# The first and last stages of a four-mixer block: input norm and final norm in the token layout, earlier parameter loads and scan operands

## The chip, the cores and the metric

One core of a Trainium2 chip. The metric is device microseconds of one execution; the kernel before takes 4182.87 us (median of 3 runs, 4181.97 to 4183.15). Everything is float32, and each matmul of that type appears in the trace as two records, a transposition as one.

## The reference

The input x has 1024 tokens of 1024 channels. The block is a long chain; only its two ends matter here:

```
h = rmsnorm(x, norm_g[0]);  proj = h @ s5_w_in;  branch, gate = split(proj)      # the head
y = s5_mixer(branch, A, log_dt, B, C, D)        # 64 groups, 64 complex states each, scan over time
x = x + ((gelu(y) * sigmoid(..)) * silu(gate)) @ s5_w_out
...                                             # gMLP, delta rule, attention, MLP, three more mixers
x = x + mixed @ w_out                           # last projection
out = rmsnorm(x, final_norm_w)                  # the tail
rmsnorm(x, g) = x * rsqrt(mean(x*x over the channels) + 1e-6) * g
```

## The kernel before

The residual lives in SBUF as `c.X`, [128 partitions, 8 blocks, 1024 tokens]: channels on the partitions. Inputs and outputs in memory have tokens in rows, so both ends are turned on TensorE. PSUM is two tensors of four banks: `products`, used as two groups of 128x1024 by turns (`start_group` waits until the group two before was read, `take_group` waits for the product, `taken` for its reading), and `others`. The engines run one written-out program each, phase after phase, with semaphores between them. SP issues the weight blocks (512 KB, eight places in a ring), ScalarE's queue the parameters and x, GpSimd's queue the scratch stores and loads and the output.

The head. ScalarE issues 13 small vector loads (L3909), then the eight tiles of x (L643), which one semaphore counts. TensorE (L654) waits for all of x and fills each product group with one block of 128 channels; ScalarE and VectorE copy the groups to `c.X` by turns (L661, L671), ScalarE squares each block (L453) and VectorE adds the squares up (L460). `rms_phase` multiplies the sum with a matrix of 1/1024 (`mean_of_total`, L489 and L493), takes Ln (L187) and Exp (L190) of 128x1024 elements and scales the eight blocks (L520). Before all that VectorE makes seven level masks (L3921 to L3928), three instructions each.

`s5_input_phase` multiplies eight blocks of the first half of `s5_w_in` (L161 in `product_ct`). TensorE first turns the state parameters' rows (L722, L723), which wait for a VectorE copy (L777) that stands behind the eight scalings. ScalarE evacuates a block (L753), GpSimd stores it to `branch_scratch` (L759). Meanwhile VectorE works out the discretised state parameters (L773 to L875) from B, C and the rest, which ScalarE's queue loads in this phase (L702 to L716).

`s5_scan_phase` has eight items. For item i VectorE makes operands (`s5_pq_done`), TensorE turns them (L985) and makes the masks' products (L997), ScalarE copies both (L1033, L1038), and TensorE needs the branch from scratch memory, in another layout, for L1006. Records of the gate's product (L962) are filled in between: one product, one product, then fourteen. GpSimd loads the branch (L926, eight DMAs per item), stores and loads the mask matrices (L940, L944). It starts on the loads of items 0 and 1 only after all eight blocks are stored, since an area of the work tensor is shared; ScalarE too waits for all eight stores before L1033.

The tail. The last projection's blocks are added to the residual (L1275), squared and summed as above; then `rms_phase` scales `c.X` in place, and `store_phase` turns it back (L3660, eight transpositions to a group), ScalarE and VectorE copy the groups by turns (L3665, L3670), and GpSimd issues the eight output tiles (L3676).

## Time and profile before

| | |
|---|---|
| median of 3 runs | 4182.87 us |
| profiled execution | 4190.77 us |
| its span, first to last instruction | 4189.0 us |
| mean granted TensorE clock | 0.97 |
| TensorE busy | 3933.0 us, 94% |
| VectorE, ScalarE, GpSimd busy | 1731.7, 895.1, 566.4 us |

A timeline row gives the start, the time from the first start to the last end of the merged instructions, the engine, the line, the operation with its tensors (output before input) and sizes, the count, and in brackets the idle time before it with what ended it. PE is TensorE's matmul, PEld its weight load, DVE VectorE, ACT ScalarE, POOL GpSimd; a q behind a name is the engine's DMA issuing. The granted clock is 1.00 at 2.4 GHz and 0.50 at 1.2 GHz.

### The profile page before, as it was taken

The page shows a single profiled execution, that of the slowest core. Times are in us where ns is not written, and L with a number is a line of the kernel's source. Part 1 is how long each engine was busy: PE and PEld are TensorE (multiplying, and loading weights), DVE is VectorE, ACT ScalarE, POOL GpSimd, SP SyncE. Part 2 cuts the span into 40 slices and gives each one's busy share as a digit, 9 for nine tenths or more (in the row PEclk, how much of TensorE's full clock was granted, in tenths as well). Part 3 has the DMA queues.
Part 4 walks back from the last instruction along what each step waited for, and adds up shares of the span by engine and source line. Part 5 has one row for each costly group of instructions (what it writes and reads, how often), then busy time and mean ns, then how long its engine had stood idle before and what let it go on. Part 6 is the DMA issues. An engine that isn't in the chain of part 4 may idle for free.

```text
span 4189.0 us, 32294 instructions
## 1 busy us (share of the span) xinstructions
PE 3933.0 (94%) x12935; PEld 1991.0 (48%) x12935; DVE 1731.7 (41%) x2512; ACT 895.1 (21%) x1033; POOL 566.4 (14%) x609
## 2 busy tenths in 40 slices
PE   5999999999899999977999999999899999899998
PEld 2455444544344776444444444444345554444553
DVE  5476433433333543144343332423445553424433
ACT  2111211111362222244130000000233430321122
POOL 0144110121000321022121221221000000000000
PEclk8998999999999999988999999999999999999998
DMA  3233111111011110200021111111101001003101
GB/s 111 79 69 84 48 40 51 40 50 41 15 35 41 26 41 16 71 21 21 10 67 44 40 50 41 40 49 42 31 26 31 26 10 46 13 13 98 31 13 43
DMA packets 291105, 174.50 MB, mean 42 GB/s; under 512 B 24095, under 2 KB 281998, under 8 KB 290702
## 3 DMA queue, kind: packets, MB, share of 16 engines
q1 hardware_dynamic: 253008, 126.47, 11.1%
q0 software_dynamic: 10000, 24.39, 2.2%
q10 hardware_dynamic: 27950, 21.58, 1.7%
q8 instruction: 104, 1.70, 0.2%
q14 instruction: 43, 0.35, 0.0%
HBM read 159.20 MB, written 13.21 MB: 41 GB/s over the span
## 4 chain that ended last, share of the span: by engine, by line
PE 54%; DVE 3%; ACT 2%; issue 1%; DMA 1%; POOL 0%; ACTq 0%; DVEq 0%
PE products L326 23%; PE products L2880 8%; PE products L161 7%; PE products L2893 3%; PE others L2959 2%; PE products L2081 1%; PE products L179 1%; PE products L534 1%; PE others L2275 1%; PE products L2244 1%; PE products L2090 1%; PE products L3408 1%; PE products L3407 1%; DMA work<-gates_scratch 1%; PE others L1492 1%
## 5 line engine op out<-in xcount | busy, mean ns | idle before, releaser
L2880 PE MATMUL products<-normed,weights 128*128 128x512 f32 (+2 forms) x704 | 318.5, 602 | 5.0 <-DVE normed L520 5.0
L161 PE MATMUL products<-normed,weights 128*128 128x512 f32 x704 | 312.5, 604 | 6.9 <-DVE s_small L3619 4.0
L326 PE MATMUL products<-gate,s_small 128*128 128x512 f32 x704 | 313.0, 592 | 0.0
L326 PE MATMUL products<-work,s_small 128*128 128x512 f32 x544 | 243.1, 593 | 0.3 <-DVE row L382 0.3
L344 POOL TENSOR_TENSOR s_small<-weights 128x512 f32<-128x512 f32 x60 | 79.5, 1325 | 1137.4 <-PE products L326 965.9
L326 PE MATMUL products<-normed,s_small 128*128 128x512 f32 x512 | 230.1, 592 | 2.3 <-DVE row L382 2.3
L356 ACT ACTIVATE s_small<-products 128x512 f32<-128x512 f32 x60 | 35.9, 599 | 861.1 <-PE products L326 861.1
L161 PEld LDWEIGHTS products<-normed,weights 128*128 128x128 f32 x704 | 135.0, 194 | 176.6 <-issue 165.3
L326 PEld LDWEIGHTS products<-gate,s_small 128*128 128x128 f32 x704 | 133.8, 190 | 168.4 <-issue 168.4
L326 PE MATMUL products<-normed,weights 128*128 128x512 f32 x448 | 203.7, 598 | 3.0 <-ACT normed L1023 3.0
L2880 PEld LDWEIGHTS products<-normed,weights 128*128 128x128 f32 (+2 forms) x704 | 125.4, 185 | 162.0 <-issue 160.3
L161 PE MATMUL products<-residual,weights 128*128 128x512 f32 x416 | 181.2, 593 | 0.9 <-ACT work L1593 0.9
L3676 POOL DMA_DIRECT2D out_dram<-work x8 | 4.3, 542 | 1210.0 <-ACT work L3665 1205.1
L326 PEld LDWEIGHTS products<-work,s_small 128*128 128x128 f32 x544 | 103.2, 190 | 130.9 <-issue 127.7
L326 PE MATMUL products<-gate,weights 128*128 128x512 f32 x352 | 160.4, 598 | 4.1 <-issue 4.1
L326 PE MATMUL products<-work,weights 128*128 128x512 f32 x320 | 147.1, 603 | 11.5 <-issue 5.8
L326 PEld LDWEIGHTS products<-normed,s_small 128*128 128x128 f32 x512 | 97.2, 190 | 125.1 <-issue 121.0
L326 PE MATMUL products<-residual,weights 128*128 128x512 f32 x320 | 144.0, 592 | 0.6 <-ACT s_small L356 0.6
L326 PEld LDWEIGHTS products<-normed,weights 128*128 128x128 f32 x448 | 85.8, 192 | 110.9 <-issue 107.6
L382 DVE TENSOR_TENSOR row<-products,s_small 128x512 f32<-128x512 f32 x60 | 41.5, 692 | 211.4 <-PE products L326 210.1
L388 DVE TENSOR_TENSOR row<-products,s_small 128x512 f32<-128x512 f32 x60 | 41.5, 692 | 209.1 <-PE products L326 207.4
L161 PEld LDWEIGHTS products<-residual,weights 128*128 128x128 f32 x416 | 78.6, 190 | 99.6 <-issue 95.7
(574 smaller groups left out, 6171.7 us busy)
## 6 DMA issues: line engine op xcount, KB each, us to landing
weights<-in_w_in_dram SPq DMA_DIRECT2D x83, 512.0 KB, 3.9
weights<-in_w_up_dram SPq DMA_DIRECT2D x32, 512.0 KB, 4.9
weights<-in_w_down_dram SPq DMA_DIRECT2D x32, 512.0 KB, 4.7
weights<-in_sgu_w_in_dram SPq DMA_DIRECT2D x24, 512.0 KB, 5.0
weights<-in_s_w_in_dram SPq DMA_DIRECT2D x16, 512.0 KB, 4.0
weights<-in_w_out_dram SPq DMA_DIRECT2D x24, 256.0 KB, 2.7
work<-in_x_dram ACTq DMA_DIRECT2D x8, 512.0 KB, 9.9
branch_scratch<-work POOLq DMA_DIRECT2D x8, 512.0 KB, 2.9
```

The costliest lines, as they stand in the source:

```text
L161: last = pe.matmul(out[0:cols, half * BANK:(half + 1) * BANK], slot(c, b, kt, cols)[:, k, :], acts[n][:, half * BANK:(half + 1) * BANK], s ...
L179: last = pe.matmul(out[:, q * P:q * P + BANK], acts[k][:, tile * P:(tile + 1) * P], wide[:, :, k, :], start=(k == 0), stop=(k == KT - 1))
L326: last = pe.matmul(bank, w[:, k * P:(k + 1) * P], moving[k], start=(k == 0 and n in (1, 3, 5)), stop=(k == KT // 2 - 1), skip_group_check= ...
L344: pool.tensor_tensor(w("S1"), w("A21"), w("A22"), ALU.add).then_inc(c.pool_step, 1)
L534: last = pe.matmul(out[:, h * BANK:(h + 1) * BANK], c.mean_mat[:, :], c.tmp[:, k % 2, h * BANK:(h + 1) * BANK], start=(k == 0), stop=(k == ...
L1492: last = pe.matmul(out[:, h * BANK:(h + 1) * BANK], c.mean_mat[:, :], squares[:, h * BANK:(h + 1) * BANK], start=True, stop=True)
L2081: last = pe.matmul(o[:, 0:BANK], slot(c, f.b, KT, P)[:, kk, :], x[kk][:, half * BANK:(half + 1) * BANK], start=(kk == 0), stop=(kk == KT - 1))
L2090: last = pe.matmul(o[:, 0:BANK], x[kk][:, f.n * P:(f.n + 1) * P], wide[:, :, kk, :], start=(kk == 0), stop=(kk == KT - 1))
L2244: pe.matmul(L[e][:, x:y], q[half(e), a, i * P:(i + 1) * P], k[half(e), a, x:y], start=True, stop=(y < w))
L2880: last = pe.matmul(out[0:cols, half * BANK:(half + 1) * BANK], slot(c, f.b, kt, cols)[:, kk, :], acts[kk][:, half * BANK:(half + 1) * BANK ...
L2893: last = pe.matmul(out[:, 0:BANK], x[kk][:, f.n * P:(f.n + 1) * P], wide[:, :, kk, :], start=(kk == 0), stop=(kk == KT - 1))
L2959: last = pe.matmul(pair(j + h)[:, i * P:(i + 1) * P], K[rows(u, h), i * P:(i + 1) * P], Q[rows(u, h), i * P:(i + 1) * P], start=True, stop ...
```

## The change

In the head, x is issued first, even tiles by SP and odd tiles by ScalarE, into another tensor (`c.C`), with one semaphore per pair. TensorE turns tile after tile (tokens, not channel blocks); VectorE makes all eight copies to `c.X`; ScalarE squares the tiles as they came in, in the token layout, each with a sum over its row, and takes Ln and Exp of the eight sums per partition. The roots are put on diagonals, and eight products with the matrix of 1/1024 spread them to a row for all partitions, which the scalings read from PSUM. The parameters' rows are loaded and turned in this phase; B and C are loaded by SP in front of weight block 2. The level masks are made behind the scalings. In the scan, the branch loads of items 0 and 1 are issued behind the store of block 5, into a free area, and ScalarE waits for seven stores only. At the end, tiles 0 and 1 are turned before the mean is known, the sums over the channels are taken by 16 products of one column, Ln and Exp have 128x8 elements, and VectorE's one pass per tile goes from PSUM to the staged output, with root and gain; the gain comes by a broadcast load. SP and GpSimd issue the stores by turns. Tiles 0, 1, 4 and 5 use the other PSUM tensor. Several private counters (of ScalarE's steps in five phases) are replaced by the common one, one for one. The core of the diff (the removed `load_phase` and `store_phase` stand above; blank lines are left out):

```diff
+def load_phase(c, x, dst, gain):
...
+    xin = c.C
+    diag = c.W[:, 10240:10240 + SEQ].rearrange("p (t n) -> p t n", n=P)
+    squares, logs, roots = (c.small[:, TT * n:TT * (n + 1)] for n in range(3))
+    rows_in = s5_rows(c)
+    par, skip = s5_par(c), c.s5.skip
+    def fetch(eng, first):
+        for t in range(first, TT, 2):
+            eng.dma_start(xin[:, t, :], x[t * P:(t + 1) * P, :]).then_inc(c.x_loaded[t // 2], 16)
...
     def tensor(pe):
         pe.wait_ge(c.consts_ready, c.n_consts)
+        for t in range(TT):
+            out = start_group(c, pe, g0 + t)
+            pe.wait_ge(c.x_loaded[t // 2], 32)
+            for k in range(KT):
+                last = pe.transpose(out[:, k * P:(k + 1) * P], xin[:, t, k * P:(k + 1) * P], c.ident[:, :])
+            last.then_inc(c.group_done, 1)
         pe.wait_ge(c.vectors_loaded, 16 * len(c.vector_rows))
         n = c.n_vector_rows
         pe.transpose(c.pb[:, 0, 0:n], c.vrows[0:n, :], c.ident[0:n, 0:n]).then_inc(c.rows_turned, 1)
+        pe.wait_ge(c.s5_rows_ready, 1)
+        pe.transpose(c.pb[:, 1, 0:96], rows_in[0:96, 0:P], c.ident[0:96, 0:96])
+        pe.transpose(c.pb[0:S5_H, 1, P:P + S5_G], rows_in[0:S5_G, P + 2:P + 2 + S5_H], c.ident[0:S5_G, 0:S5_G])\
+          .then_inc(c.rows_turned, 1)
+        out = start_group(c, pe, g_row)
+        for t in range(TT):
+            pe.wait_ge(c.scaled, scaled + t + 1)
+            last = pe.matmul(out[:, t * P:(t + 1) * P], c.mean_mat[:, :], diag[:, t, :], start=True, stop=True)
+        last.then_inc(c.group_done, 1)
+    def scalar(act):
+        act.wait_ge(c.consts_ready, c.n_consts)
+        act.activation(logs[:, 0:1], c.eps_rms, ACT.Ln)
+        for t in range(TT):
+            act.wait_ge(c.x_loaded[t // 2], 32)
+            ins = act.activation(dst[:, t, :], xin[:, t, :], ACT.Square, accum_out=squares[:, t:t + 1])
+        act_step(c, ins, "x_squares")
+        act.wait_ge(c.act_step, c.act_at["x_squares"])
+        act_step(c, act.activation(logs, squares, ACT.Ln, scale=1.0 / D_MODEL, bias=c.eps_rms), "x_logs")
+        act.wait_ge(c.act_step, c.act_at["x_logs"])
+        act_step(c, act.activation(roots, logs, ACT.Exp, scale=-0.5), "x_roots")
+    def vector(dve):
+        ch = c.dve_chain
+        for t in range(TT):
+            if t == TT - 2:
+                dve.wait_ge(c.s5_rows_loaded, 64)
+                ch.done(dve.tensor_copy(rows_in[64:96, 0:P].rearrange("j (e p) -> j e p", e=2),
+                                        rows_in[64:96, P:P + 2].unsqueeze(2).broadcast_to([32, 2, S5_P])), c.s5_rows_ready)
+            dve.tensor_copy(c.X[:, :, t * P:(t + 1) * P], take_group(c, dve, g0 + t).rearrange("p (k n) -> p k n", n=P))\
+               .then_inc(c.group_read[(g0 + t) % 2], 1)
+        dve.wait_ge(c.rows_turned, 1)
+        ch.done(dve.tensor_copy(c.vecs[:, 0:c.n_vector_rows], c.pb[:, 0, 0:c.n_vector_rows]))
+        dve.wait_ge(c.act_step, c.act_at["x_roots"])
+        for t in range(TT):
+            dve.tensor_scalar(diag[:, t, :], c.ident[:, :], roots[:, t:t + 1], float(D_MODEL), ALU.mult, ALU.mult)\
+               .then_inc(c.scaled, 1)
+        dve.wait_ge(c.rows_turned, 2)
+        ch.done(dve.tensor_copy(par.rearrange("p a j -> p (a j)"), c.pb[:, 1, 0:96]), c.s5_rows_ready)
+        ch.done(dve.tensor_copy(skip[0:S5_H, :], c.pb[0:S5_H, 1, P:P + S5_G]))
+        row = take_group(c, dve, g_row)
+        taken(c, dve, g0 + TT - 1)
+        taken(c, dve, g0 + TT - 2)
+        ch.wait()
         for k in range(KT):
+            ins = dve.scalar_tensor_tensor(dst[:, k, :], c.X[:, k, :], gain[:, k:k + 1], row, ALU.mult, ALU.mult)
+            ch.done(ins, c.normed)
+        ch.done(dve.memset(c.small[:, 63:64], 0.0), c.group_read[g_row % 2], g_row // 2 + 1)
+    phase = Phase(tensor=tensor, scalar=scalar, vector=vector)
+    phase.fetch, phase.normed = fetch, normed
...
+    def fetch_rows(sp):
...
+    def fetch(sp):
         for e in range(2):
...
-        for k in range(4):
-            pool.wait_ge(c.branch_stored[k], 32)
+            if m == KT - 3:
+                phase.early(pool)
...
-    U = [area(GC, S5_N)]
+    U = [c.W[:, 13056:13056 + GC * S5_N].rearrange("p (a b) -> p a b", a=GC)]
+    at[0] += GC * S5_N
...
+        pool.wait_ge(c.branch_stored[i % 4], 16 * (i // 4 + 1))
...
+    def early(pool):
+        pool.wait_ge(c.s5_pq_done, 1)
+        load_branch(pool, 0)
+        load_branch(pool, 1)
+    before.early = early
     def gpsimd(pool):
-        pool.wait_ge(c.s5_pq_done, 1)
+        pool.wait_ge(c.branch_stored[3], 32)
         pool.memset(within[:, :, :], 0.0).then_inc(c.pool_step, 1)
         pool.wait_ge(c.pool_step, POOL_FIRST)
-        load_branch(pool, 0)
         for i in range(S5_C):
             if i >= 1:
                 pool.wait_ge(c.s5_y_done, i)
-            if i + 1 < S5_C:
-                load_branch(pool, i + 1)
+                if i + 1 < S5_C:
+                    load_branch(pool, i + 1)
...
-        for k in range(4):
+        for k in range(3):
...
+def final_phase(c, src, gain, out, sums, free):
+    g_mean = c.plan.groups
+    c.plan.groups += 1
+    spare = [i for i in range(TT) if i % 4 < 2]
+    g = {}
+    for i in range(TT):
+        if i not in spare:
+            g[i] = c.plan.groups
+            c.plan.groups += 1
+    scaled = c.n_scaled
+    c.n_scaled += len(spare)
+    stage, gains = c.D, c.B[:, 0, :]
+    logs, roots = (c.small[:, TT * n:TT * (n + 1)] for n in range(2))
+    row_no = {i: ROWS_TURNED + n + 1 for n, i in enumerate(spare)}
+    def pair(i):
+        return c.pb[:, 2 * (i % 4):2 * (i % 4) + 2, :].rearrange("p a n -> p (a n)")
+    def fetch(sp):
+        sp.wait_ge(c.group_done, free + 1)
+        sp.dma_start(gains, gain.partition_broadcast(P)).then_inc(c.params_loaded, 16)
     def tensor(pe):
+        tile, sem, value = sums.last
+        def turn(i, first, last):
+            to = pair(i) if i in spare else c.pa[:, (g[i] % 2) * SEQ:(g[i] % 2 + 1) * SEQ]
+            for k in range(first, last):
+                ins = pe.transpose(to[:, k * P:(k + 1) * P], src[:, k, i * P:(i + 1) * P], c.ident[:, :])
+            return ins
+        pe.wait_ge(c.collected, sums.collected + KT - 2)
+        for i in spare[0:2]:
+            turn(i, 0, KT - 1)
+        taken(c, pe, g_mean - 1)
+        for i in spare[0:2]:
+            turn(i, KT - 1, KT).then_inc(c.rows_turned, 1)
+        means = start_group(c, pe, g_mean)
+        pe.wait_ge(sem, value)
         for i in range(TT):
+            pe.matmul(means[:, i:i + 1], sums.total[:, i * P:(i + 1) * P], c.mean_mat[:, 0:1], start=True, stop=False)
+            last = pe.matmul(means[:, i:i + 1], tile[:, i * P:(i + 1) * P], c.mean_mat[:, 0:1], start=False, stop=True)
+        last.then_inc(c.group_done, 1)
+        for i in range(2, TT):
+            if i in spare:
+                pe.wait_ge(c.scaled, scaled + spare.index(i) - 1)
+                turn(i, 0, KT).then_inc(c.rows_turned, 1)
+            else:
+                start_group(c, pe, g[i])
+                turn(i, 0, KT).then_inc(c.group_done, 1)
     def scalar(act):
+        act_step(c, act.activation(logs, take_group(c, act, g_mean)[:, 0:TT], ACT.Ln, bias=c.eps_rms), "final_logs")
+        act.wait_ge(c.act_step, c.act_at["final_logs"])
+        act.activation(roots, logs, ACT.Exp, scale=-0.5).then_inc(c.group_read[g_mean % 2], 1)
     def vector(dve):
+        dve.wait_ge(c.params_loaded, loaded("final"))
+        taken(c, dve, g_mean)
         for i in range(TT):
+            if i in spare:
+                dve.wait_ge(c.rows_turned, row_no[i])
+                got, sem = pair(i), c.scaled
+            else:
+                got, sem = take_group(c, dve, g[i]), c.group_read[g[i] % 2]
+            dve.scalar_tensor_tensor(stage[:, i, :], got, roots[:, i:i + 1], gains, ALU.mult, ALU.mult).then_inc(sem, 1)
+    def store(eng, first):
+        for i in range(first, TT, 2):
+            if i in spare:
+                eng.wait_ge(c.scaled, scaled + spare.index(i) + 1)
+            else:
+                taken(c, eng, g[i])
+            eng.dma_start(out[i * P:(i + 1) * P, :], stage[:, i, :]).then_inc(c.out_stored[first], 16)
+        eng.wait_ge(c.out_stored[first], 16 * TT // 2)
+    def gpsimd(pool):
+        store(pool, 1)
+    def sync(sp):
+        fetch(sp)
+        store(sp, 0)
...
+        load = then(load_phase(c, t["x"][0], c.B, c.vec["norm_g0"]))
+        s5_in = then(s5_input_phase(c, t, load.normed))
+        scan = then(s5_scan_phase(c, t, s5_in))
...
-        norm = then(rms_phase(c, c.X, c.X, c.vec["final_norm_w_3"], sums=sums))
-        then(store_phase(c, c.X, out[0], norm.normed))
+        ml = then(mlstm_phase(c, t, sums))
+        final = then(final_phase(c, c.X, t["final_norm_w_3"], out[0], sums, ml.last_projection))
...
+            load.fetch(sp, 0)
             for n, (src, kt, cols, _) in enumerate(c.plan.blocks):
+                if n == 2:
+                    s5_in.fetch(sp)
...
+            final.sync(sp)
...
+            load.fetch(act, 1)
+            s5_in.fetch_rows(act)
...
+            phases[0].vector(dve)
...
-                phase.vector(dve)
+                if k:
+                    phase.vector(dve)
```

## Rows read from the trace of the kernel before

**Rows 1.** The page, busy time (share of the span) and instructions.

```profile
...
PE 3933.0 (94%) x12935; PEld 1991.0 (48%) x12935; DVE 1731.7 (41%) x2512; ACT 895.1 (21%) x1033; POOL 566.4 (14%) x609
...
```

**Rows 2.** Timeline, 0 to 62 us: start, duration, engine, line, idle before.

```profile
...
8.80 0.29 DVE L3928 TENSOR_TENSOR levels<-levels,triu 128x128 f32<-128x128 f32 x1
9.43 1.28 ACT L661 ACT_TABLE_LOAD   x1 [9.43 <-issue]
...
22.85 4.69 PE L654 MATMUL products<-ident,work 128*128 128x128 f32 x24 [11.51 <-DMA work<-in_x_dram]
...
26.56 1.23 DVE L671 COPY residual<-products 128x1024 f32<-128x1024 f32 x1 [14.84 <-PE products L654]
...
31.43 2.00 ACT L453 ACTIVATE work<-residual 128x1024 f32<-128x1024 f32 x2 [1.64 <-DVE work L460]
...
51.33 9.66 DVE L520 SCALAR_TENSOR_TENSOR normed<-residual,vectors,row 128x1024 f32<-128x1024 f32 x8 [10.39 <-ACT row L190]
...
54.49 1.53 ACTq L711 DMA_DIRECT2D work<-in_s_B_im_dram  x1
56.05 5.79 ACTq L716 DMA_DIRECT2D work<-in_s_C_re_dram  x8
61.01 0.22 DVE L777 COPY work<-work 32x128 f32<-32x128 f32 x1
...
61.84 48.62 PE L161 MATMUL products<-normed,weights 128*128 128x512 f32 x106
...
```

**Rows 3.** DMA queues from 0 to 50 us: packets, MB, share of 16 engines.

```profile
...
q10 hardware_dynamic: 1377, 4.26, 22.2%
...
```

**Rows 4.** Busy time of five engines, granted clock, DMA share, GB/s.

```profile
...
66.00:68.00 2.00, 2.00 (x4) 0.86 (x3) 0.32 (x2) 0.23 (x1) 0.00 (x0) 0.59 0.22 49
...
```

**Rows 5.** Timeline, 140 to 207 us.

```profile
...
142.84 0.42 DVE L1112 COPY work<-s_small 128x512 f32<-128x512 f32 x1
...
180.68 1.13 PE L962 MATMUL products<-normed,weights 128*128 128x512 f32 x2
182.55 1.02 ACT L1033 ACTIVATE work<-others 128x1024 f32<-128x1024 f32 x1 [3.35 <-DMA branch_scratch<-work]
...
183.84 8.39 POOL L926 DMA_DIRECT2D work<-branch_scratch  x16 [0.29 <-POOL work L931]
...
190.24 3.68 PE L1006 MATMUL others<-work 128*64 128x128 f32 x32 [8.43 <-DMA work<-branch_scratch]
...
193.85 12.31 PE L962 MATMUL products<-normed,weights 128*128 128x512 f32 x28
...
194.68 4.19 POOL L944 DMA_DIRECT2D work<-within_scratch  x8 [1.96 <-DMA within_scratch<-work]
...
```

**Rows 6.** Timeline, 4150 us to the end.

```profile
...
4153.54 3.57 PE L489 MATMUL products<-work,mean_mat 128*128 128x512 f32 x4 [2.54 <-DVE work L460]
...
4156.95 1.88 PE L493 MATMUL products<-work,mean_mat 128*128 128x512 f32 x4
...
4162.39 9.66 DVE L520 SCALAR_TENSOR_TENSOR residual<-residual,vectors,row 128x1024 f32<-128x1024 f32 x8 [8.99 <-ACT row L190]
...
4172.10 6.33 PE L3660 MATMUL products<-ident,residual 128*128 128x128 f32 x33 [0.72 <-DVE residual L520]
...
4174.26 0.61 POOL L3676 DMA_DIRECT2D out_dram<-work  x1 [1204.12 <-ACT work L3665]
...
4178.87 1.97 PE L3660 MATMUL products<-ident,residual 128*128 128x128 f32 x16 [0.44 <-DVE work L3670]
...
4182.41 1.22 DVE L3670 COPY work<-products 128x1024 f32<-128x1024 f32 x1 [1.19 <-PE products L3660]
...
```

**Rows 7.** Windows at the end, columns as in rows 4.

```profile
...
4186.00:4187.00 1.00, 0.00 (x0) 0.00 (x0) 0.00 (x0) 0.00 (x0) 0.00 (x0) 0.50 1.01 410
...
```

**Rows 8.** ScalarE's groups by line: count, busy us, mean ns, idle before.

```profile
...
L190 ACT ACT_TABLE_LOAD x32 | 41.1, 1283 | 0.6
...
```

**Rows 9.** Line 3346: durations in ns, first and last start.

```profile
...
L3346 PE MATMUL others<-ident,work x8: 249/249/271, 3725.1 to 3725.9; 8*128 8x8 f32 x8
...
```

More of the change, by code:

```diff
@@ L874, in vector, with s5_scan_phase @@
             m *= 2
-    return Phase(loads=loads, tensor=tensor, scalar=scalar, vector=vector, gpsimd=gpsimd)
-def s5_scan_phase(c, t):
+    phase = Phase(tensor=tensor, scalar=scalar, vector=vector, gpsimd=gpsimd)
+    phase.fetch, phase.fetch_rows, phase.early = fetch, fetch_rows, nothing
+    return phase
+def s5_scan_phase(c, t, before):
     g0 = c.plan.groups
@@ L3850, in then @@
             return phase
-        load = then(load_phase(c, t["x"][0]))
-        norm = then(rms_phase(c, c.X, c.B, c.vec["norm_g0"], sums=load.sums))
-        then(s5_input_phase(c, t, norm.normed))
-        scan = then(s5_scan_phase(c, t))
+        load = then(load_phase(c, t["x"][0], c.B, c.vec["norm_g0"]))
+        s5_in = then(s5_input_phase(c, t, load.normed))
+        scan = then(s5_scan_phase(c, t, s5_in))
         gate = then(s5_gate_phase(c, t, scan))
```

155 lines of the change are left out of this document (53 added, 102 removed).

## The prediction

> **What bounds the kernel now.** I read the page first: TensorE is busy 94% of the span [rows 1], so an edit away from TensorE is worth something only where TensorE waits. Then the timeline of the first 62 us. The reader is to see that the products of the first projection start at 61.84 and that everything before is one chain [rows 2]: x is issued behind the thirteen parameter loads on ScalarE's queue and is waited for as a whole (first transposes at 22.85), then transposes and evacuations by channel block, squares, a mean over 1024 columns, Ln and Exp over 128x1024, eight scalings on VectorE (51.33 to 60.99), and last a small copy at 61.01 that the state parameters wait for behind those eight. Third, the timeline from 140 to 207: one hole of 8.43 us before L1006, released by the load of the branch from scratch memory [rows 5]. Fourth, the tail: TensorE is through with the projection at about 4150.4, and 38.6 us of summing, scaling, turning and storing follow to 4189.0 [rows 6, 7]. So three holes, and the middle moves as a block.
>
> **The head, step by step.** New order: x goes first, its even tiles on SP's queue and its odd ones on ScalarE's, waited for in pairs. In the first 50 us ScalarE's queue (nearly all of it x) took 22.2% of the engines' time [rows 3], 11.1 us; weights no longer share that time, because the first ones stand behind x on SP. From a first packet at 2.2 us (an estimate: 1.4 us after the first issue) x is in at 13.3 and its semaphore at about 14.6, the pairs 2.8 us apart before that. ScalarE issues 20 DMAs instead of 21 before its table load, which sat at 9.43 [rows 2]: load from 9.2, a tiny Ln, squares from 10.9. Eight squares at 1.00 each (two in 2.00, [rows 2]) end at 19.0; the last pair of x (14.6) doesn't hold them up. The sum per token that each square now also gives is an operation no row shows. I price it between nothing and another 1.00 each, as if it were an instruction of its own (8.0 in all), and take nothing, because the square passes over the same 1024 elements. VectorE's eight evacuations at 1.23 [rows 2] start at about 8.5 and end by 19.0, beside the squares. Ln over 128x8: 0.25. The Exp brings its own table again, 1.28 [rows 8], and 0.25: 20.8. Eight diagonals of 128x128 at 0.26 (rows of that size take 0.29 and overlap slightly, [rows 2]): 22.9. The last of eight 128x128 products: 23.2; the two parameter copies lie beside it. First scaling, 9.66/8 = 1.21: 24.5. The first product starts there, not at 61.84: **37.3 us earlier**. It need not wait again: a channel block costs TensorE four records of 0.43 and VectorE 1.21. The low clock stays: in the window from 66 to 68 the mean was 0.59, so the clock rose at 67.6, after 5.8 us of products at half speed, 2.9 us lost [rows 4]; I leave these in, since TensorE again has some idle microseconds before. Bounds of the head: with x as late as before (22.85, then two squares and the same steps, first product 30.4) 31.4 us; with the squares twice as dear, 29.3; with no slow start and the steps from 20.8 to 24.5 at half their price, 42.0.
>
> Behind it: the seven level masks (21 instructions, the last at 8.80; at 0.29 each 6.1 us, [rows 2]) now stand between the scalings and the state parameters. VectorE needs the operands of the first scan item (they were ready at 142.8, 81 us after the first product, [rows 5]); of that 75 were VectorE's own chain, estimated from 67.6, where its first step stood behind ScalarE. Now it is 8.5 for the other seven scalings, 6.1 and 75, 90 us after the first product, and TensorE asks for them before 180.68, 116 us after it: 26 us of cover, so nothing. GpSimd now waits for them too, ahead of its last two stores: it arrives there 90 us after the first product and the next store is due 13.7 us later (a block of 32 records at 0.43), which covers the 8.4 of issuing [rows 5]. The 20 parameter loads (four with 64-byte pieces, 16 smaller) move to SP, ahead of weight blocks 2 to 7. On ScalarE the loads took up to 1.53 each and 5.79 for eight [rows 2]: 4 x 1.53 + 2 x 5.79 = 17.7 us. Block 2 is issued by about 25 and needed 27.5 us after the first product, at 52. Nothing.
>
> **The scan.** The first two loads of the branch are issued after the store of block 5 instead of after that of block 7; 16 issues took 8.39 us from 183.84 [rows 5]. What is late next? TensorE is through with its filler at 180.68 + 1.13 = 181.81. ScalarE's two copies (1.02 and 1.00) no longer wait for the last store (3.35 us idle before, [rows 5]); they need only the transposes and the small products that end as L962 begins at 180.68, so the second ends at about 181.8 also. L1006 starts at 181.85 instead of 190.24: 8.4. It also took 3.68 at the low clock after the hole; without the hole half, so 1.8 more, of which I count 1.7, since a last part was at the full one. GpSimd's next loads must be in when the filler of 12.31 behind L1006 ends, at 196.1: last store landed at 182.55, then memset, a store and its return (10.84 from the start of the branch loads to that of these, less the 8.39: 2.5), eight loads (4.19, [rows 5]) and landing: 193. VectorE's path to the states starts from L1006's end as before and moves with it. **10.1 us**; 7 if these loads come to bind (3 us later than I have them), 10.1 at most.
>
> **The tail.** TensorE starts at 4153.54 as before (behind the same last sum on VectorE). It turns tiles 0 and 1 first: 16 transposes at 0.22 (33 in 6.33 less the wait, [rows 6]; low clock, as L489 shows) to 4157.0. Then the sums by token: 16 products of one column, two records each. No row has one column; the nearest, eight of eight columns, begin 0.11 apart [rows 9]; 32 x 0.11 = 3.6 to 4160.7 at the full clock, 7.0 at the low one. Before, the mean ended at 4158.83, so this step loses 1.9. ScalarE gains it back: two 128x1024 activations (1.11 + 1.06) become two of 0.25, the table load between them stays: 4162.5, where VectorE began before too (4162.39). But that pass now goes from PSUM straight to the staged output: eight at 1.23 end at 4172.3, where the last evacuation ended at 4183.63. Stores: before, the first was issued at 4174.26 and moved bytes from 4175.4; now the first tile is ready at 4163.75, so bytes from about 4165.4. 4.19 MB at the rate of the last windows (410 GB/s with the engines full, [rows 7]; 395 is my estimate over all) are 10.6 us: 4176.0, and the 1.8 us that followed the last byte before: 4177.9. By the last tile alone: 4172.3 + 5.37 = 4177.7. **11.0 us**; bounds 5 (everything at the low clock) and 13 (one-column products at half the price).
>
> The Trainium skill, DMA: Bandwidth & Descriptors, section Issuing engines are not separate DMA queues, says that issuing from several engines saves only the sequencer's time, as the transfers share 16 engines. The trace agrees (engines full and 410 GB/s with one queue, [rows 7]), and by that rule the second store queue by itself is worth nothing; the gain is the earlier first store. The skill's ScalarE: Activation LUTs, section Table sets, has a set that holds both exp and ln; by it one table load would go, 1.3 us at each end. Here all 32 Exps behind an Ln load again [rows 8], so I keep them; by the page the sum would be 61.0 and the median 4121.9.
>
> **Sum.** 37.3 + 10.1 + 11.0 = 58.4. The profiled execution: 4190.8 - 58.4 = 4132.4 (span 4189.0 to 4130.6). It lay 7.9 above the median of the runs, 4182.87; the median becomes 4124.5. What a measurement of this kernel can tell from no change is 0.2%, 8.4 us.
>
> **The rivals.** (A) x does not land sooner: with two queues and the small parameter loads in between, the last pair comes as late as before. For it: the engines were already full up to 23 us. Against it: half of those bytes were weights. The first product at 30.4: 4130.4. (B) Transposes and one-column products do not bring the clock up. Then the tail stays low from 4153.5: sums 3.4 us longer, and a tile's eight transposes 1.8 to 2.0 instead of 1.1 against VectorE's 1.23, 2.4 more: 5.8, so 4130.3. The Trainium skill, TensorE: Matmul & The Clock Gate, part 4, says just this, that transposes don't count as busy for the gate. Against it: from 4172.1 on the trace has only transposes, and the last 16 took 1.97 us, 0.12 each, against 0.22 at first [rows 6]. (C) The scan's hole closes only in part, as GpSimd, now waiting for VectorE before its last stores, or the loads of the mask matrix end last: 3 us back, 4127.5; a full return of it, 4134.6. (D) Slower than before: the parameter loads block the weight stream. SP issues in order, and 20 loads of small pieces now sit before block 2. For it: one such load held ScalarE's queue up to 1.53, where a tile of x takes under half. Against it: 17.7 us in all. From the point where block 2 lands later than 52 us each microsecond of it is one of TensorE's, and the first 58 only eat the gain, so the loads would have to take 102 us; at 115, block 2 lands at 123: 4124.5 + 71 = 4195.5. (E) The edits don't do what they say, for instance the scan's operands come late and the head's gain turns into a wait at 177: 4175 to 4183.
>
> **Chances.** Forecast 0.62, A 0.14, B 0.10, C 0.07, E 0.03, D 0.04, of which 0.03 slower. A, B and C differ in a few microseconds and can add up (4142). Range 4116 to 4142: the low end is 42.0 + 10.1 + 13 = 65 and 2 for the runs' spread, the high end 31.4 + 7 + 5 = 43 less 2. Faster 0.95, same 0.02, slower 0.03.
>
> **What would show it.** Right: the first L161 near 24.5; evacuations and squares done near 19; no wait before L1006, and it at 2 us; VectorE's last pass starting about 9 us after the last residual sum, pitch 1.23, and the end 5.5 us after it. Wrong: squares or copies spaced by the DMA beyond 16 us; a table load between squares; TensorE waiting for VectorE or GpSimd near 140 us; transposes at 0.22 in the tail; a gap between VectorE's last eight.

## The result, and the profile after

The changed kernel takes 4113.0 us (median of 4 runs, 4112.6 to 4118.6) against 4183.0 for the one before beside it (4 runs, 4182.0 to 4190.0): 0.9832 of it, 95% interval 0.9815 to 0.9849. The gain is 70.0 us where 58.4 were forecast, and 4113.0 lies 3 us below the low end of the range. Over all occasions of this study after has a mean of 4119.3 (14 executions, 4112.4 to 4129.4, standard deviation 6.4) and before one of 4185.0 (51 executions, 4171.7 to 4194.3, deviation 5.2, one reading of 4317.9 at a granted clock of 0.926 left out): a gain of 65.7, plus or minus 3.7 at 95% (twice the root of 6.4²/14 + 5.2²/51). That is the number to explain; 4119.3 lies inside the range, so the miss of the range itself is the luck of the first four executions. The interval is rather narrow: two sets of executions of the same program before, taken side by side, have means of 4182.1 (10) and 4187.4 (14).

The page of after, first part, answers to [rows 1]: 27 us fewer of TensorE's busy time.

```profile
PE 3906.0 (95%) x12967; PEld 1982.8 (48%) x12967; DVE 1723.9 (42%) x2515; ACT 882.8 (21%) x1033; POOL 559.8 (14%) x605
```

**The head** (timeline of after; columns as in [rows 2], a q is DMA issuing):

```profile
5.82 6.36 PE L664 MATMUL products<-ident,gate 128*128 128x128 f32 x32 [5.82 <-DMA gate<-in_x_dram]
7.88 1.23 DVE L698 COPY residual<-products 128x1024 f32<-128x1024 f32 x1 [7.88 <-PE products L664]
9.66 1.28 ACT L681 ACT_TABLE_LOAD   x1 [9.66 <-issue]
11.06 1.04 ACT L684 ACTIVATE normed<-gate 128x1024 f32<-128x1024 f32 x1
12.01 0.19 ACT L684 ACTIVATION_READ_ACCUMULATOR normed<-gate 128x1 f32 x1
...
19.28 0.19 ACT L684 ACTIVATION_READ_ACCUMULATOR normed<-gate 128x1 f32 x1
19.82 1.28 ACT L689 ACT_TABLE_LOAD   x1
21.36 1.66 DVE L704 TENSOR_SCALAR work<-ident,small 128x128 f32<-128x128 f32 x8 [2.58 <-ACT small L689]
21.79 3.54 PE L676 MATMUL products<-work,mean_mat 128*128 128x128 f32 x16 [4.34 <-DVE work L704]
25.37 4.85 DVE L714 SCALAR_TENSOR_TENSOR normed<-residual,vectors,products 128x1024 f32<-128x1024 f32 x4 [2.07 <-PE products L676]
26.80 3.67 PE L161 MATMUL products<-normed,weights 128*128 128x512 f32 x8 [1.46 <-DVE normed L714]
```

The squares end at 19.5, half a microsecond after the forecast (19.0), and Exp and diagonals follow on time. Then the sixteen records of the row product (L676) take 3.54 us, 0.22 each, at the low clock, and the first projection starts at 26.80, not 24.5. Windows of after (us, busy time of the five engines with instructions, granted clock, DMA share, GB/s) show what makes up for part of that:

```profile
22.00:24.00 2.00, 2.00 (x10) 2.00 (x11) 1.30 (x8) 0.23 (x1) 0.00 (x0) 0.50 0.93 90
24.00:25.00 1.00, 1.00 (x7) 1.00 (x6) 0.00 (x0) 0.00 (x0) 0.00 (x0) 0.51 0.53 87
25.00:26.00 1.00, 0.33 (x3) 0.14 (x2) 0.63 (x1) 0.00 (x0) 0.00 (x0) 1.00 0.16 36
```

The clock rises on the row products. So L161 starts at 1.00 here, and the 2.9 us of slow start, which the forecast had left in [rows 4], are gone in this execution. They are not gone in every one. Two later profiles of the same kernel have the low clock behind L161's start, which is at 27.05 and 27.21 there (one window of each):

```profile
27.00:30.00 3.00, 2.95 (x4) 1.43 (x5) 3.00 (x3) 0.00 (x0) 0.00 (x0) 0.50 0.26 60
27.20:30.20 3.00, 2.99 (x4) 1.45 (x5) 3.00 (x3) 0.00 (x0) 0.00 (x0) 0.50 0.23 53
```

There the clock had fallen at 19.9 and 20.4, ahead of the row products, and came back at 30.1 and 30.6, where in the first profile it fell at 21.6 and was back at 25.0.

**The scan** (timeline of after, answers to [rows 5]):

```profile
142.71 1.13 PE L1016 MATMUL products<-normed,weights 128*128 128x512 f32 x2
142.83 1.01 ACT L1092 ACTIVATE work<-others 16x1024 f32<-16x1024 f32 x1 [0.75 <-PE others L1051]
143.90 1.97 PE L1060 MATMUL others<-work 128*64 128x128 f32 x32
145.05 0.95 POOL L986 MEMSET work<- 128x1024 f32 x1 [2.97 <-DMA branch_scratch<-work]
145.80 12.28 PE L1016 MATMUL products<-normed,weights 128*128 128x512 f32 x28
148.74 4.21 POOL L998 DMA_DIRECT2D work<-within_scratch  x8 [1.95 <-DMA within_scratch<-work]
```

L1060 (L1006 before) has no wait and takes 1.97 instead of 3.68. The fourteen products behind it (the 28 records of the row at 145.80) start at 145.80 instead of 193.85: 48.05 us earlier.

**The tail** (timeline of after, answers to [rows 6]):

```profile
4084.27 1.23 DVE L1329 TENSOR_TENSOR residual<-products,residual 128x1024 f32<-128x1024 f32 x1 [4.51 <-PE products L161]
4086.69 3.58 PE L3738 MATMUL others<-ident,residual 128*128 128x128 f32 x16 [2.45 <-DVE work L460]
4090.06 0.38 PE L3750 MATMUL products<-mean_mat,work 128*128 128x1 f32 x2
...
4093.43 0.36 PE L3751 MATMUL products<-mean_mat,work 128*128 128x1 f32 x2
4094.11 1.28 ACT L3764 ACT_TABLE_LOAD   x1
4095.70 2.48 DVE L3775 SCALAR_TENSOR_TENSOR work<-others,small,normed 128x1024 f32<-128x1024 f32 x2 [9.07 <-ACT small L3764]
4097.02 7.48 SPq L3783 DMA_DIRECT2D out_dram<-work  x4
4097.27 2.06 PE L3738 MATMUL others<-ident,residual 128*128 128x128 f32 x16
...
4102.86 2.47 DVE L3775 SCALAR_TENSOR_TENSOR work<-products,small,normed 128x1024 f32<-128x1024 f32 x2
...
4105.62 0.53 POOL L3783 DMA_DIRECT2D out_dram<-work  x1 [1.85 <-DVE work L3775]
```

From the last residual sum to the end of the span (4110.8) it is 26.5 us, where it was 37.96 (4151.04 to 4189.0): 11.4 less. Both ends together: 48.05 + 11.4 = **59.5**, one over the forecast.

That is the first pair of profiles. Four profiles of this study have the head and scan of before (before twice, the tail alone twice) and three are of after; their means are, in us:

```
                                             before's head (4)   after (3)   gain
first L161                                        61.63            27.02    34.61
first transposes of the scan                     177.29           141.20    36.09
a mark in the scan (a table load, L1111)         214.78           168.73    46.05
last residual sum to the end, old and new tail    37.99            26.62    11.37
```

By these the ends give 46.05 + 11.37 = **57.4**, and about 8 of the 65.7 us lie between the mark and the tail, where the edits did little but put the common counter of ScalarE's steps in the place of private ones.

### The profile page after: what moved, and what is told of

It is laid out like the page before. It is cut to its first block, busy times and chain, and to the rows that moved or that the text cites. A ratio compares the mean times of both kernels' runs of the same rounds, so it can differ in the third digit from the quotient of the medians.

```text
span 4110.8 us, 32365 instructions
## 1 busy us (share of the span) xinstructions
PE 3906.0 (95%) x12967; PEld 1982.8 (48%) x12967; DVE 1723.9 (42%) x2515; ACT 882.8 (21%) x1033; POOL 559.8 (14%) x605
## 4 chain that ended last, share of the span: by engine, by line
PE 55%; ACT 2%; DVE 2%; issue 1%; DMA 0%; POOL 0%; ACTq 0%; DVEq 0%
PE products L326 23%; PE products L2934 8%; PE products L161 7%; PE products L2947 3%; PE others L3013 2%; PE products L2135 1%; PE products L179 1%; PE products L534 1%; PE products L2298 1%; PE others L2329 1%; PE products L2144 1%; PE products L3462 1%; PE products L3461 1%; PE others L1546 1%; PE others L3046 1%
## 5 line engine op out<-in xcount | busy, mean ns | idle before, releaser
L161 PE MATMUL products<-normed,weights 128*128 128x512 f32 x704 | 309.8, 600 | 8.4 <-DVE s_small L3673 4.0
L161 PEld LDWEIGHTS products<-normed,weights 128*128 128x128 f32 x704 | 134.0, 192 | 176.5 <-issue 164.8
L161 PE MATMUL products<-residual,weights 128*128 128x512 f32 x416 | 181.2, 593 | 0.9 <-ACT work L1647 0.9
L326 PE MATMUL products<-work,weights 128*128 128x512 f32 x320 | 147.3, 603 | 11.5 <-issue 5.8
L161 PEld LDWEIGHTS products<-residual,weights 128*128 128x128 f32 x416 | 78.6, 190 | 99.6 <-issue 95.8
```

The lines of the kernel that those rows point to most:

```text
L161: last = pe.matmul(out[0:cols, half * BANK:(half + 1) * BANK], slot(c, b, kt, cols)[:, k, :], acts[n][:, half * BANK:(half + 1) * BANK], s ...
L326: last = pe.matmul(bank, w[:, k * P:(k + 1) * P], moving[k], start=(k == 0 and n in (1, 3, 5)), stop=(k == KT // 2 - 1), skip_group_check= ...
```

## The experiments

Two things were open: does each edit give what its term says, and where does the rest come from? Theory one (drift) for the rest: TensorE's low-clock stretches in the middle fall differently in each execution, and only their mean counts. Theory two (start): they depend on when the middle starts, so after has a mean of its own. (In the recorded expectations drift is N, R or C, start is P or O, and D is a third theory: an edit outside the ends speeds the middle.) Medians, and means where executions are pooled, are of each kernel's own executions.

**The kernel before, unchanged.**

> The kernel before, unchanged, profiled once more, to learn what of its first profile is its own. The changed kernel gained 70.0 us in the median; the two ends (head and scan 48.05, tail 11.4) give 59.5, and between them the profiles differ by 18.7 more, of which 7.9 is what the profiled execution of before lay above its median. Theory P (phase of the clock: the stretches of low clock in the middle depend on when the middle starts): the attention stage, from its first L2306 to the next stage's squares, takes the same time as in the first profile within 1 us, and the 12 us of low clock in the scan near 320 us are either there (then about 4190) or not (then about 4183). Theory N (the difference is chance of single executions): the attention stage comes out several us shorter or longer.

Median 4184.7 over 10 executions (4171.7 to 4189.0; those of before beside it 4178.1 to 4194.3), ratio 0.9988 [0.9976, 1.0]. The same program moves by 20 us from one execution to the next, far more than the 0.2% that I took from three close readings. The profiled one of them has the stage lengths of the first profile within 0.4 us (the attention stage 306.3 and 306.4), so the two profiles alone would have spoken against drift.

**The new tail alone.**

```diff
-        norm = then(rms_phase(c, c.X, c.X, c.vec["final_norm_w_3"], sums=sums))
-        then(store_phase(c, c.X, out[0], norm.normed))
+        final = then(final_phase(c, c.X, t["final_norm_w_3"], out[0], sums, ml.last_projection))
```

> Before with the new last phase alone (and one of the private counters replaced, to have a semaphore for it). The middle then starts when it did. Tail's own price from the profiles: 11.4. Theory P: 4183.0 - 11.4 = 4171.6, within 1. Theory D (an edit outside the ends, such as the shared counters or the shorter program, speeds the middle itself): 4161 to 4171.

Median 4165.7 (5 executions), ratio 0.9954 [0.9938, 0.9971]: 19 us, against 11.4. Its tail is 26.6 long, 11.4 shorter than before, as it should be. The rest came from the middle, although the program up to 4131 us is that of before but for one counter in the last mixer.

**The changed kernel without the early branch loads.**

```diff
-            if m == KT - 3:
-                phase.early(pool)
...
-        pool.wait_ge(c.branch_stored[3], 32)
+        for k in range(4):
+            pool.wait_ge(c.branch_stored[k], 32)
```

> The changed kernel with the branch loads of items 0 and 1 issued after all eight stores again, as before. The scan's hole should return: L1006's counterpart about 8.4 us later and at the low clock, 10.1 in all. Theory D and N: 4113.0 + 10.1 = 4123.1. Theory P: the middle starts 10.1 us later than in the changed kernel, so its low-clock stretches fall differently and the median lies 3 us or more from 4123.1 in either direction.

The timeline of this kernel has the hole back, and the load of the branch in front of it:

```profile
146.25 8.39 POOL L971 DMA_DIRECT2D work<-branch_scratch  x16 [0.29 <-POOL work L985]
152.63 3.68 PE L1060 MATMUL others<-work 128*64 128x128 f32 x32 [8.61 <-DMA work<-branch_scratch]
156.24 13.23 PE L1016 MATMUL products<-normed,weights 128*128 128x512 f32 x28
```

The fourteen products start at 156.24 instead of 145.80: 10.4, the term of 10.1. But the median is 4139.6, ratio 0.9895 [0.988, 0.9909]: 20 us above after's mean. Half of that is the hole, half came later.

**The changed kernel with VectorE held for four memsets before its first scalings.** The diff, here with 4; the runs below take 1 and 8:

```diff
+        for _ in range(4):
+            ch.wait()
+            ch.done(dve.memset(c.W[:, 12288:13312], 0.0))
         for k in range(KT):
```

> The changed kernel with four memsets of 128x1024 on VectorE in front of the first scalings: every later stage has the same instructions and starts d later, d being what the profile shows for the four (2 to 4 us). Theory D and N: 4113.0 + d. Theory P: the distance to 4113.0 is not d but several us off it, and the attention stage's length has changed.

L161 starts at 31.77, 4.97 later, and at the low clock, which lasts from 28.4 to 35.2. At the mark in the scan it is 6.7 us behind the first profile of after and 5.4 behind the mean of three. Median 4132.9, ratio 0.9873 [0.9856, 0.9889]; the mean is 12.2 above after's.

**The changed kernel again, with one memset, and with all stores on one queue.** These ran beside each other.

> The changed kernel, unchanged, in more executions, beside the next three kernels on the same chip. The delayed kernel came out 20 us later than the first runs of this one for a delay of 5, and all of it beyond the head lay in stages with more time at the low clock. Theory P (where the middle starts decides where the clock falls): these executions agree with the first four, 4112.6 to 4118.6. Theory R (each execution draws its own low-clock stretches, whatever the start): they spread over some 10 to 20 us, as the executions of before did next to the last four kernels (4171.7 to 4194.3), and their median lies above 4113, at 4115 to 4130.

> The changed kernel with one memset in front of the first scalings: all later stages start about 1.2 us later. Theory R: the median of e5 + 1.2, within 4. Theory P: 5 us or more off that, and about the same in every execution.

> The changed kernel with all eight output tiles issued by GpSimd. If the DMA engines are what the stores wait for, as the prediction has it, the end moves by no more than 0.6 us in the last phase (from the last residual add to the end of the span: 26.5 us in the changed kernel). If the second queue has a worth of its own, 1.5 us or more.

After: 4118.0 (4112.4 to 4129.4), ratio 0.9849 [0.9827, 0.9871]. One memset: L161 at 28.00; median 4122.8 (4113.0 to 4133.1), ratio 0.9857 [0.9836, 0.9879]; not to be told from after. One queue:

```diff
-        store(pool, 1)
+        for i in range(TT):
...
+            pool.dma_start(out[i * P:(i + 1) * P, :], stage[:, i, :]).then_inc(c.out_stored[0], 16)
```

4122.6, ratio 0.9852 [0.9834, 0.987]. Its tail, from the last residual sum at 4095.93 to the end at 4123.3, is 27.4, 0.8 longer than after's; the nine other profiles with this tail lie between 26.56 and 26.65. So the second queue is worth 0.8 of the 11.4, between the two values that were set against each other (0.6 at most, 1.5 at least). The first store is issued at 4109.35, 1.9 behind the start of VectorE's first pass, where SP issued it 1.3 behind. The Trainium skill, DMA: Bandwidth & Descriptors, section Issuing engines are not separate DMA queues, says that several issuing engines save the sequencer's time alone; this trace agrees: 0.6 of the 0.8 are the later first issue.

**A faster version.** The twelve vector loads go from ScalarE's queue to GpSimd's, VectorE's copy of the gains goes behind the diagonals, and the first tiles of the tail are turned ahead of the last residual sum:

```diff
-                act.dma_start(c.vrows[n * KT:(n + 1) * KT, :], src).then_inc(c.vectors_loaded, 16)
+                pool.dma_start(c.vrows[n * KT:(n + 1) * KT, :], src).then_inc(c.vectors_loaded, 16)
...
-        pe.wait_ge(c.collected, sums.collected + KT - 2)
+        taken(c, pe, g_mean - 2)
```

> The changed kernel with three edits. The twelve vector loads are issued by GpSimd, so that ScalarE's squares begin at about 6.7 instead of 11.06; the vectors' copy stands behind the diagonals; and at the end TensorE turns blocks 0 to 6 of tiles 0 and 1 as soon as those blocks are added, not after the last sum. Expected from the profile: roots at 18.5 instead of 21.3, the eight row products at the full clock because TensorE pauses only 1.5 us, first product at about 21.9 instead of 26.80 (4.9 us); in the tail the sums by token start at 4.1 us and not at 5.8 us after the last residual add's end, at the full clock, 3.5 us in all. Together 8.4 below e5, if the middle moves as a block; up to 10 off that by the middle's clock.

Timeline and one window of this kernel:

```profile
5.28 1.28 ACT L681 ACT_TABLE_LOAD   x1 [5.28 <-issue]
18.93 2.02 PE L676 MATMUL products<-work,mean_mat 128*128 128x128 f32 x16 [1.63 <-DVE work L702]
22.42 1.96 PE L161 MATMUL products<-normed,weights 128*128 128x512 f32 x4 [1.47 <-DVE normed L713]
...
4080.22 1.92 PE L3737 MATMUL others<-ident,residual 128*128 128x128 f32 x16
4080.42 1.23 DVE L1328 TENSOR_TENSOR residual<-products,residual 128x1024 f32<-128x1024 f32 x1 [4.51 <-PE products L161]
```
```profile
22.40:24.00 1.60, 1.58 (x4) 0.86 (x5) 1.60 (x2) 0.00 (x0) 0.00 (x0) 1.00 0.72 91
```

The table load is 4.4 us sooner, since ScalarE no longer issues the twelve first; the row products run at the full clock (2.02 instead of 3.54), and L161 starts at 22.42, 4.4 before after's. TensorE had paused 1.63 us before them, against 4.3 to 4.5 in the profiles of after, and the clock didn't fall. In the tail the sixteen transposes run in the shadow of the residual sum, and 23.5 us follow it instead of 26.5. By the ends it is 7.4 faster than after. Measured: 4112.8 (4 executions), ratio 0.9829 [0.9809, 0.985], mean 6.6 below after's. Its interval overlaps that of after in the same group, so the trace shows the gain at the ends and the times only don't contradict it.

**Repeats, and the start moved.** These four ran beside each other: after, the tail alone, before with four memsets ahead of its first scalings, and after with eight.

> The kernel after, unchanged, on another occasion. Open is the part of the gain that the two ends do not give: nine executions of after have a mean of 4117.7, 37 of before one of 4184.6, and the ends account for 59.5 (4125.1). Chance (C): the low-clock stretches in the middle are drawn anew by each execution, sd 6, and the nine were lucky: the mean of these five is 4125 plus or minus 5. Own draw of each program (O): after really loses less in the middle: 4118 plus or minus 5, and the stretch from item 0 of the scan to 430 us again 263 to 265 long, not 271.6 as in both profiles of before.

> The new tail alone, again. Up to 4150 us its program is that of before, so theory O, in its form in which what matters is when the middle starts, has no reason to differ from 4184.6 - 11.4 = 4173.2. Chance (C): mean 4173 plus or minus 5, and the first five (mean 4166.0) were lucky. If it comes to 4166 again, neither the start time nor the edits at the ends explain a program's mean, and a difference between programs of some 7 us exists that no edit makes.

> The kernel before with four VectorE memsets of 128x1024 in front of its first scalings (1.2 us each, 4.8 in all): everything behind them starts 4.8 us later. Chance (C): 4184.6 + 4.8 = 4189.4 plus or minus 5. Start time decides (O with phase): the low-clock stretches of the middle fall elsewhere, so the mean is off that by 5 us or more in either direction, and the profile's stretch up to 430 us is 265 instead of 271.6 long.

> After with eight such memsets before its first scalings (9.6 us; one cost about 1.2 and four 5.2 at the first product, and the slow start of 1.5 to 2.9 us comes back). Chance (C), from 4125.1: 4125.1 + 9.6 + 2 = 4137 plus or minus 5. From after's own mean of 4117.7: 4129 plus or minus 5. With the scan's loads and masks unchanged, nothing else should move.

| kernel | median, us | ratio |
|---|---|---|
| after | 4121.9 (5) | 0.9846 [0.9831, 0.986] |
| tail alone | 4172.0 (5) | 0.9964 [0.9951, 0.9977] |
| before, 4 memsets | 4184.3 (11) | 0.9996 [0.9987, 1.0005] |
| after, 8 memsets | 4140.1 (4) | 0.9885 [0.9871, 0.9899] |

The same program, the tail alone, now has 4172.0 where it had 4165.7: drift is real. But drift alone sits badly with two findings. Before with four memsets starts its projection at 66.05 instead of 61.84, 4.2 later, and its mean (4184.4) lies 0.6 below that of before (4185.0), plus or minus 2.2: a delay on TensorE's path cost nothing in the mean. And each delay of after cost more than itself: with one, four and eight memsets, and without the early loads, the mark in the scan (the table load of ScalarE, at 168.7 on average of three profiles of after) stands 1.6, 5.4, 11.1 and 10.1 us later, and the means are 5.1, 12.2, 19.3 and 20.7 above after's 4119.3. Each mean of four or five is good to some 6 us, so no single one of these decides; that all four lie on one side speaks for theory two, but doesn't show it. The two that ran beside after exceed its mean there by 4.1 (one memset) and 16.5 (eight), for 1.6 and 11.1 at the mark; the other two had no after beside them. And one profile speaks against the start alone: the kernel with one queue has after's program up to the tail and passes the mark at 167.8, where after passed it at 167.4, yet takes 4.1 us more from the scan's end to the attention stage and 8.2 more in that.

**What differs in the middle.** The stage from 167 to 437 us of after (most of the scan, matched by ScalarE's instructions) was measured in the profile of each kernel:

```
profile             length, us   TensorE busy at the low clock, us
before                 277.4        33.2
before again           277.4        33.0
tail alone, 1st        271.3        17.4
tail alone, 2nd        277.5        33.2
before, 4 memsets      273.0        23.4
after (three)      269.3 to 270.4   17.4
six other variants 268.7 to 271.4   17.4 to 20.9
```

The two profiles of the tail alone, the same program, show where the 6 us sit. First the second of them, then the first (timelines, TensorE):

```profile
317.99 0.46 PE L1016 MATMUL others<-work 128*128 128x128 f32 x2 [0.62 <-DMA work<-within_scratch]
...
320.49 1.11 PE L1018 MATMUL others<-work 64*128 64x128 f32 x4
321.53 0.79 PE L1016 MATMUL others<-work 128*128 128x128 f32 x2
322.25 1.22 PE L1018 MATMUL others<-work 64*128 64x128 f32 x4
```
```profile
315.76 0.46 PE L1016 MATMUL others<-work 128*128 128x128 f32 x2 [0.72 <-DMA work<-within_scratch]
...
319.96 0.49 PE L1016 MATMUL others<-work 128*128 128x128 f32 x2
320.38 0.71 PE L1018 MATMUL others<-work 64*128 64x128 f32 x4
```

and their windows, in the same order:

```profile
322.00:330.00 8.00, 8.00 (x27) 5.98 (x27) 4.78 (x12) 0.00 (x0) 0.00 (x0) 0.50 0.00 1
```
```profile
320.00:324.00 4.00, 4.00 (x25) 3.15 (x24) 3.69 (x10) 0.00 (x0) 0.00 (x0) 1.00 0.00 0
```

Both wait 0.6 to 0.7 us for GpSimd's mask loads; in one the clock falls 2.7 us later and a pair of rows takes 1.87 us, in the other nothing follows and it takes 1.06. In after the same products (L1070, at 268.68) have no wait in front of them, as the item's loads came earlier relative to TensorE. The kernel without the early branch loads shows which edit did that, since its wait is back:

```profile
280.94 0.46 PE L1070 MATMUL others<-work 128*128 128x128 f32 x2 [0.71 <-DMA work<-within_scratch]
```

Six profiles have this wait, 0.56 to 0.81 us: in three of them (0.56, 0.64, 0.62) the clock fell behind it and stayed low for 13.7 us, in three (0.72, 0.81, 0.71) it didn't. Of the eight in which the branch loads are early, seven have no such wait and one has 0.31, and the clock fell in none. So the scan's edit also took away the occasion for this stretch. The attention stage (1718 to 2014 us of after) is the other place: three profiles of after, one program, take 296.2, 300.8 and 306.6 there. Its windows for the first and the third:

```profile
1718.30:2014.50 296.20, 245.42 (x1024) 126.56 (x1021) 129.84 (x280) 99.66 (x195) 69.25 (x80) 0.94 0.06 18
```
```profile
1717.40:2024.00 306.60, 253.65 (x1024) 128.44 (x1021) 129.96 (x280) 99.48 (x195) 69.04 (x80) 0.92 0.06 18
```

The same 1024 records are busy 8.2 us longer at a clock of 0.92 instead of 0.94 (the second window runs to 2024.0, as the stage does). From 2014 to 4085 us all fourteen profiles of this study agree within 1.0 us (2070.4 to 2071.4).

## Why the prediction was right in direction and too small

**The head: right in sum, by two errors of opposite sign.** Squares, copies and Exp came within 0.6 us of their times (19.5, 18.6 and 21.3 against 19.0, 19.0 and 20.8). The sum per token costs a read of 0.19 us behind each square, most of it covered: the pitch is 1.04 instead of 1.00, so it was right to take nothing of the 8.0. Mis-sized was the row product: "the last of eight products: 23.2" took it at the full clock, it ran at the low one and ended at 25.3 (2.1 more, and 0.2 with the scaling). Mis-sized the other way was "the low clock stays", 2.9 us. In the first profile the row products brought the clock up, and the path gained 35.0 by start times and 38.0 where both kernels have the full clock again (the transposes of the first scan item, 177.85 before, 139.88 after). The term was 37.3; that these came so close is luck. With after's head unchanged L161 started at the full clock in three of five profiles (after's first, one queue, no early loads) and at the low one, for some 3 us more, in two, and the mean gain at the transposes is 36.1. Around these lie the version with GpSimd's loads, whose clock never fell, and the memsets: with one the clock fell again at 28.3, with four at 28.4, and with eight it stayed low from before the row products until 41.7.

Rival A fell too: from 12.49 on the transposes wait for VectorE's copies and not for x, which ScalarE's squares don't wait for either; what held them was the table load behind twenty issues (9.66, forecast 9.2).

**The scan: right.** 10.1 forecast, 48.05 - 37.97 = 10.08 found, 10.44 when put back alone. No wait for the mask loads took its place (rival C), from L161's start to the branch's products TensorE waits for neither VectorE nor GpSimd (rival E), and SP's twenty loads, from 8.97 to 32.8, delayed no weights (rival D): 23.8 us instead of 17.7, still before the 52 at which block 2 was due.

**The tail: right.** 11.0 forecast, 11.4 found. Measured from the last residual sum: transposes to 5.8 (forecast 6.0), one-column products to 9.4 (9.7), first scaling at 11.4 (11.5), last one done at 21.1 (21.3), end at 26.5 (26.9). (The 4150.4 from which the prediction counts 38.6 us is the start of the last product; from the residual sum it is 38.0, and no term used it.) The pitch of the one-column records is 0.112, as that of the eight-column ones [rows 9].

**Rival B fell.** The tail doesn't stay low. Its one-column products ran at the full clock from 4090.3 on; after them it has transposes alone, and the clock fell at 4093.7 and rose again in them at 4097.1 (windows of after):

```profile
4093.70:4095.70 2.00, 1.93 (x10) 1.53 (x10) 0.00 (x0) 1.76 (x3) 0.00 (x0) 0.50 0.00 0
4097.30:4099.30 2.00, 2.00 (x18) 1.62 (x15) 2.00 (x3) 0.00 (x0) 0.50 (x1) 1.00 0.65 262
```

The Trainium skill, TensorE: Matmul & The Clock Gate, part 4, says that transposes don't count as busy for the gate. In the kernel before, TensorE has nothing but transposes from 4163.8 us on, and the clock, low from 4163.6, rises in the row of 33 records at 4177.3 (windows of before):

```profile
4172.10:4177.10 5.00, 5.00 (x24) 4.99 (x25) 1.22 (x1) 2.05 (x2) 1.15 (x2) 0.50 0.29 117
4178.87:4182.37 3.50, 3.05 (x24) 2.58 (x24) 1.23 (x1) 1.64 (x2) 1.77 (x4) 1.00 0.85 339
```

So for float32 transposes of 128x128 the measurement decides against it.

**The step that failed: "the middle moves as a block".** The edits' own gain is 57.4 (59.5 in the first pair of profiles), close to the 58.4, but the middle is not a block of fixed length. It holds stretches at the low clock behind short waits, and these fall differently in each execution (20 us between the slowest and the fastest execution of one program); that they also depend on when the stage starts is likely, not shown. Of the 8 us over the ends' sum (65.7 less 57.4, plus or minus 3.7 by the times alone), the scan stage gives most by the profiles: three of four with before's head have its long form and none of nine with the new one, and 0.75 x 6.2 (277.5 - 271.3) is 4.7. That count is small, and why the clock falls after a wait of 0.62 and not after one of 0.72 stays open.

How much of the 8 us the edits made stays open too. The tail alone is the check: its middle is before's, yet its ten executions have a mean of 4168.8, 16.2 below before (plus or minus 3.9), 4.8 more than its 11.4. A rest of that order thus appears where no edit of the head or scan can have made it. Nor does a run change the private counters alone. What the four memsets in before show is only that a few microseconds of start time can leave the mean where it was.

The rest of the 70.0 is the luck of four executions (mean 4114.3, where later ones of the same kernel had 4121.2). I also took 0.2% as what a measurement can tell, from three readings 1.2 us apart, and put 2 us of spread into the range; the deviation of one execution is 5 to 6, and the 7.9 by which the profiled execution lay above the median was such a draw and no property of profiling. The high end of the range took 31.4 for the head, although the dearer squares gave 29.3; that did not come to bear.

## What to carry to other kernels

Sum an edit's gain on the path from trace to trace, between two marks around the edit, and treat the rest of the difference as a question of its own: compare the granted clock and the length of each untouched stage in several executions before giving it a cause. When TensorE waits a few microseconds, small products just before the big ones may bring the clock up in the shadow of another engine; here they did in three of five profiles, and with one, four or eight memsets more between them the big ones had the low clock at or just behind their start. A shorter pause before the small products did better: 1.63 us instead of 4.3 to 4.5, and the clock didn't fall in the one profile of that version. An engine that must issue DMAs before its first computation starts that much later; the queue of an idle engine is the place for them.

## What the runs showed of the hardware beyond that

- An ACTIVATE with a sum over its row is followed by a read of the accumulator of 0.19 us, but the next one starts 1.04 us behind the last, for 1024 elements, against 1.00 without.
- Issuing small loads was dearest right behind two weight blocks on the same queue: SP took 4.37 and 5.25 us for the first two loads of B in after (8.97 to 18.6), 1.40 and 1.53 for the next two.
- One-column float32 products begin 0.112 us apart per record, like those of eight columns.
- A wait of 0.6 to 0.8 us in the scan was followed by the low clock in three profiles and not in three others (the tail alone, one program, had it once and once not); one such stretch cost 6 us, ten times the wait.
